# First block of a two-block transformer kernel: the first projections read tokens to which the adaptation shift is not yet added, weight units come in another order, and projections and adaptation parts are placed between the attention heads

## The reference, cut to what matters

```
c_act = silu(c)
ada = c_act @ w_ada + b_ada                    # six parts of 1024
shift_a, scale_a, gate_a, shift_m, scale_m, gate_m = split(ada, 6)
h = rmsnorm(x, g_mix) * (1 + scale_a) + shift_a
gq, gk, gv, gr, gg, mq, mk, mv = split(h @ w_in, ...)   # 256 256 512 512 16 512 512 512
log_a = log_sigmoid(gg @ w_gla_gate + b_gla_gate) / 16
o_gla = rmsnorm(gated_linear_attention(gq, gk, gv, log_a)) * silu(gr)   # 4 heads
o_moba = causal_attention(mq, mk, mv, rel_bias)          # 8 heads of 64
x = x + gate_a * (concat(o_gla, o_moba) @ w_out)
h = rmsnorm(x, g_mlp) * (1 + scale_m) + shift_m
x = x + gate_m * (square(relu(h @ w_ff1)) @ w_ff2)
```

## Time and profile before

| | |
|---|---|
| median of three runs | 1892.06 us |
| the profiled execution | 1894.33 us, its span 1892.2 us |
| PE busy | 1411.1 us (75%) |
| DVE, ACT, POOL busy | 273.4, 237.9, 37.0 us |
| bytes moved | 649.02 MB, mean 343 GB/s |
| first product of `gg` | 41.40 us |
| first scores of the head loop | 145.40 us |
| first product of the output projection | 199.46 us |
| first product of the feed-forward part | 237.60 us |
| last expert | up to the end of the span |

### The profile page before, as it was taken

The page is one execution under the profiler, slowest core; times in us unless marked ns, Lnnn a source line. Parts: engine busy times, 40 slices in busy tenths (PEclk is TensorE's granted clock), DMA queues, the critical chain, the costliest instruction groups (busy, mean ns, idle before and its releaser), DMA issues.

```text
span 1892.2 us, 23896 instructions
## 1 busy us (share of the span) xinstructions
PE 1411.1 (75%) x10492; PEld 824.8 (44%) x10492; DVE 273.4 (14%) x539; ACT 237.9 (13%) x529; POOL 37.0 (2%) x63
## 2 busy tenths in 40 slices
PE   5997899999999776756666676586667658466665
PEld 2674688888857332322323233242232323223222
DVE  1115200003971210010100001000010000101001
ACT  2223122102122310100001000000100001000010
POOL 0000000000110000000000000000000000000000
PEclk8998899999999688677767767767776776776777
DMA  9358233244242899999999999999999999999998
GB/s 350 150 194 343 107 156 155 112 178 155 90 182 93 336 410 427 440 427 437 431 426 438 431 430 435 428 432 436 430 430 434 431 429 439 427 432 435 423 437 344
DMA packets 47207, 649.02 MB, mean 343 GB/s; under 512 B 3816, under 2 KB 6320, under 8 KB 30016
## 3 DMA queue, kind: packets, MB, share of 16 engines
q1 hardware_dynamic: 44112, 643.90, 80.6%
q10 hardware_dynamic: 2848, 3.55, 0.5%
q0 software_dynamic: 208, 1.00, 0.1%
HBM read 647.38 MB, written 1.06 MB: 343 GB/s over the span
## 4 chain that ended last, share of the span: by engine, by line
DMA 49%; PE 20%; DVE 1%; issue 0%; ACT 0%; POOL 0%; SPq 0%; DVEq 0%; PEldq 0%; ACTq 0%; POOLq 0%
DMA ring<-in_w 49%; PE ps L1131 20%; DVE xT L1123 0%; DVE small L1029 0%; DVE arena L1079 0%; DVE arena L1081 0%; DVE arena L1025 0%; ACT L678 0%; ACT L666 0%; POOL arena L446 0%; SPq L359 0%; DVE arena L1098 0%; ACT arena L666 0%; PE ps L1630 0%; ACT arena L719 0%
## 5 line engine op out<-in xcount | busy, mean ns | idle before, releaser
L1131 PE MATMUL ps<-ring,table 128*32 128x352 f32 x4032 | 475.6, 627 | 244.6 <-DMA ring<-in_w 244.4
L1131 PEld LDWEIGHTS ps<-ring,table 128*32 128x32 f32 x4032 | 142.8, 139 | 464.7 <-DMA ring<-in_w 240.2
L1131 PE MATMUL ps<-ring,arena 128*32 128x256 f32 (+1 forms) x2818 | 197.5, 438 | 151.6 <-DMA ring<-in_w 144.0
L1131 PEld LDWEIGHTS ps<-ring,arena 128*32 128x32 f32 (+1 forms) x2818 | 102.9, 125 | 247.5 <-issue 143.1
L1131 PE MATMUL ps<-hT,ring 128*128 128x256 f32 (+1 forms) x912 | 200.4, 382 | 6.8 <-ACT hT L600 3.5
L1131 PEld LDWEIGHTS ps<-hT,ring 128*128 128x128 f32 (+1 forms) x912 | 171.5, 189 | 35.8 <-issue 9.3
L1131 PE MATMUL ps<-arena,ring 128*128 128x256 f32 x768 | 173.0, 387 | 4.4 <-POOL arena L446 2.4
L1131 PEld LDWEIGHTS ps<-arena,ring 128*128 128x128 f32 x768 | 148.4, 194 | 27.8 <-issue 4.2
L1131 PEld LDWEIGHTS ps<-arena,hT 128*128 128x128 f32 x512 | 101.4, 282 | 103.9 <-issue 103.9
L1131 PE MATMUL ps<-arena 32*128 32x256 f32 (+10 forms) x532 | 97.7, 382 | 27.7 <-DVE xT L1123 12.2
L1131 PE MATMUL ps<-arena,hT 128*128 (+1 forms) x512 | 115.6, 366 | 1.8 <-DVEq L1107 1.8
(11 more groups left out here) (213 smaller groups left out, 514.3 us busy)
## 6 DMA issues: line engine op xcount, KB each, us to landing
ring<-in_w SPq DMA_DIRECT2D x76, 5632.0 KB, 32.2
ring<-in_w SPq DMA_DIRECT2D x19, 2816.0 KB, 29.0
ring<-in_w SPq DMA_DIRECT2D x35, 1408.0 KB, 32.7
ring<-in_w_ff SPq DMA_DIRECT2D x8, 4096.0 KB, 13.1
ring<-in_w_ada SPq DMA_DIRECT2D x6, 4096.0 KB, 14.0
ring<-in_w_in SPq DMA_DIRECT2D x4, 4096.0 KB, 17.8
ring<-in_w_out SPq DMA_DIRECT2D x2, 4096.0 KB, 13.9
ring<-in_w_in SPq DMA_DIRECT2D x3, 2048.0 KB, 10.6
```

The source lines that it names most:

```text
L1131: return pe.matmul(o, w, x, start=first, stop=last)
```

## The change

The position of units and of labels (the list `FREED` gives the order in which PE frees the units):

```diff
-UNITS = (["ada0", "ada1", "win_a", "win_b", "win_c", "win_d", "ada2", "ada3", "ada4", "ada5", "wout"]
+UNITS = (["ada1", "win_a", "ada0", "win_v", "ada2", "win_c", "ada3", "win_r", "ada4", "wout", "ada5"]
+FREED = ["ada1", "ada0", "win_a", "win_v", "ada2", "win_c", "win_r", "ada3", "ada4"] + UNITS[9:]
+FILLER = {0: "gr1", 1: "gr2", 2: "gr3", 3: "ada3", 4: "at3", 5: "ada4", 6: "at4"}
-    order = ["rel", "n_in", "ada0", "at0", "ada1", "at1", "gg", "gq0", "gq1", "gk0", "gk1", "z"]
-    order += [f"wf{i}" for i in range(4)] + ["gv0", "gv1"] + [f"gr{i}" for i in range(4)]
-    order += [f"mq{i}" for i in range(4)] + [f"mk{i}" for i in range(4)]
-    order += ["klT", "att0", "att1", "kv0", "kv1", "mv0", "mv1", "o0", "o1", "gs0", "gs1"]
+    order = ["n_in", "ada1", "at1", "gg", "gq0", "gq1", "rel", "ada0", "gk0", "at0", "gk1", "bias", "gv0", "bt", "gv1", "z"]
+    held = {label: set(order[order.index(label) + 1:order.index("bt") + 1]) for label in ("gg", "gq0", "gq1", "gk0", "gk1")}
+    held["gv0"] = {"bt"}
+    order += [f"wf{i}" for i in range(4)] + ["mv0", "mv1", "ada2", "mq0", "at2"]
+    order += [f"mq{i}" for i in range(1, 4)] + [f"mk{i}" for i in range(4)]
+    order += ["klT", "att0", "att1", "kv0", "kv1", "gr0", "o0", "o1", "gs0", "gs1"]
```

SP no longer waits for the small inputs; the values' columns come in two pieces; small inputs have semaphores of their own, and x is waited for only before its squares:

```diff
-            sp.wait_ge(s["small_in"], 16 * 8)
...
-                    sp.wait_ge(s["unit_used"], i - 2)
+                    sp.wait_ge(s["unit_used"], FREED.index(UNITS[i - 3]) + 1)
...
+                if name == "win_v":
+                    sp.dma_start(unit[:, :, n:], rows(T["w_in"], 2576, 512)).then_inc(s["mv_in"], 16)
```

ACT adds the shift to `hT` only after `gk1`, adds a computed bias when it empties the first five banks, and reads `relR` back after them; `gr` is emptied later, inside the head loop:

```diff
-            act.dma_start(rel_dram, rtb).then_inc(s["rel_dram_in"], 16)
-            act.wait_ge(s["rel_dram_in"], 16)
-            act.dma_start(relR, bass.AP(rel_dram.tensor, 0, [[1, P], [384, MH], [1, S]])).then_inc(s["relW_in"], 16)
+            act.dma_start(rel_dram, rtb).then_inc(s["relW_in"], 16)
+            act.wait_ge(s["relW_in"], 16)
+
+            act.wait_ge(s["shift_set"], 1)
+            wait_filled(act, "gk1")
             for c in range(C):
-                act.wait_ge(s["t0_set"], c + 1)
                 A(hT[:, c, :], hT[:, c, :], ACT.Identity, bias=ada[:, c:c + 1]).then_inc(s["hT_set"], 1)
...
+            act.wait_ge(s["gbias_set"], 1)
+            take("gg", ggT, bk("gg")[0:RANK, 0:S], s["ggT_set"], 1, ACT.Identity, bias=gbias[0:RANK, 4:5])
+            for k, label in enumerate(("gq0", "gq1", "gk0", "gk1")):
+                take(label, (gq, gk)[k // 2][:, k % 2 * S:(k % 2 + 1) * S], bk(label)[:, 0:S], s["gqk_set"], k + 1,
+                     ACT.Identity, bias=gbias[:, k:k + 1])
+            act.dma_start(relR, bass.AP(rel_dram.tensor, 0, [[1, P], [384, MH], [1, S]])).then_inc(s["relW_in"], 16)
+            take("gv0", gv[:, 0, :], bk("gv0"), s["gv_set"], 1)
```

PE:

```diff
-            proj("gg", wg, 0, hT, s["hT_set"], n=RANK)
+            proj("gg", wg, 0, hT, s["t0_set"], n=RANK)
             proj("gq0", w, 0, hT)
             proj("gq1", w, P, hT)
+            pe.wait_ge(s["rest_in"], 16 * 4)
+            inc_filled(mm(bk("rel")[0:MH, 0:384], relst, onehot, True, True), "rel")
+            ada_part(0)
             proj("gk0", w, 2 * P, hT)
-            proj("gk1", w, 3 * P, hT, last=True)
+            ada_turn(0)
+            proj("gk1", w, 3 * P, hT)
+            pe.wait_ge(s["shift_set"], 1)
+            wait_emptied(pe, "bias")
+            for c in range(C):
+                mm(bk("bias")[0:32, P:P + RANK], ada[:, c:c + 1].broadcast_to([P, 32]), wg[:, c, :], c == 0, c == C - 1)
+            for c in range(C):
+                for j in range(4):
+                    ins = mm(bk("bias")[32 * j:32 * j + 32, 0:P], ada[:, c:c + 1].broadcast_to([P, 32]),
+                             w[:, c, j * P:(j + 1) * P], c == 0, c == C - 1)
+            finish("bias", ins)
+            wait_unit(pe, "win_v")
+            w = unit_ap("win_v", C, 1024)
+            proj_rows("gv0", w, 0, hT, 0, wait=s["hT_set"])
...
+            pe.transpose(bk("bt")[:, 0:P], rowb[:, 0:P], ident[:, :])
+            inc_filled(pe.transpose(bk("bt")[0:RANK, P:P + 32], rowb[0:32, P:P + RANK], ident[0:32, 0:32]), "bt")
+            proj_rows("gv1", w, 0, hT, 1)
             pe.wait_ge(s["ggT_set"], 1)
...
-            pe.wait_ge(s["relW_in"], 16)
+            pe.wait_ge(s["relW_in"], 32)
             for i in range(4):
                 wait_emptied(pe, f"wf{i}")
...
+            pe.wait_ge(s["mv_in"], 16)
             for st in range(ST):
+                proj_rows(f"mv{st}", w, 512, hT, st, last=(st == 1))
+            ada_part(2)
```

DVE: the order is `ada_rows(1)`, `ada_cols(1)`, the eight chunks of `hT`, then part 0, then two copies each for `bias` and `bt`; the relative table is multiplied by 8 when `wf` is copied. In the head loop scale, add and maximum become one operation:

```diff
-                    V.scalar_tensor_tensor(scb[:, b, 0:P], bk(f"sc{i}")[:, 0:P], HD ** -0.5, relW[:, i, P:2 * P],
-                                           ALU.mult, ALU.add)
...
-                    V.reduce_max(mx[:, 0:1], scb[:, b, 0:P], AX.X)
-                    link(V.reduce_max(mx[:, 1:2], scb[:, b, P:P + S], AX.X))
+                    for st, a, n in ((0, 0, P), (1, P, S)):
+                        ins = V.tensor_tensor_reduce(scb[:, b, a:a + n], bk(f"sc{i}")[:, a:a + n],
+                                                     relW[:, i, P - a:P - a + n], HD ** -0.5, NEG, ALU.add, ALU.max,
+                                                     mx[:, st:st + 1])
```

More of the change, by code:

```diff
@@ L76, in bank_plan @@
             order.append(f"pv{i // 2 - 1}")
-    order += ["n_mlp"] + [f"y{m}" for m in range(C)] + [f"f{m}" for m in range(FF // P)]
-    held = {"n_mlp": {f"y{m}" for m in range(C)}}
+    order += ["n_mlp"] + [f"y{m}" for m in range(C)] + ["ada5", "f0", "f1", "at5"]
+    order += [f"f{m}" for m in range(2, FF // P)]
+    held["n_mlp"] = {f"y{m}" for m in range(C)} | {"ada5"}
     order += [f"g{m}" for m in range(C)] + ["qk0", "n_fin", "qk1"]
@@ L194, in build @@
         h1 = ar(0, 8192, m=FF // P)
-        relst = arena[0:BUCKETS, 4736:4744]
+        relst = arena[0:BUCKETS, 14336:14344]
+        rowb = ar(14344, P + RANK)
+        gbias = small[:, 80:85]
         relW = ex(0, 2048, h=MH)
@@ L517, in take @@
                 empty(act, label)
[L519 to L523, removed]
+            act.wait_ge(s["gbias_set"], 1)
[5 more added lines that the diff above has]
+            take("gv0", gv[:, 0, :], bk("gv0"), s["gv_set"], 1)
+            take("gv1", gv[:, 1, :], bk("gv1"), s["gv_set"], 2)
             wait_filled(act, "z")
@@ L534, in _ @@
             A(tt, tt, ACT.Ln, bias=1.0).then_inc(s["zl_set"], 1)
[L535 to L541, removed]
-            A(flat(sgr), flat(gr), ACT.Sigmoid).then_inc(s["sgr_set"], 1)
             act.wait_ge(s["b_set"], 3)
@@ L587, in _ @@
                           accum_out=rsum[:, 2 * b + st:2 * b + st + 1]).then_inc(s["exp_set"], 1)
+                if i < 3:
+                    gr_take(i + 1)
+                if i == 5:
+                    A(flat(sgr), flat(gr), ACT.Sigmoid).then_inc(s["sgr_set"], 1)
                 if i >= 1:
@@ L757, in ada_cols @@
                 empty(dve, f"at{k}")
-            for k in range(2):
-                ada_rows(k)
-                ada_cols(k)
+            dve.wait_ge(s["x_in"], 16)
+            ada_rows(1)
+            ada_cols(1)
             g0 = VEC["g_mix"][0]
@@ L768, in _ @@
                     .then_inc(s["t0_set"], 1)
+            ada_rows(0)
+            ada_cols(0)
+            dve.sem_inc(s["shift_set"], 1)
+            wait_filled(dve, "bias")
+            V.tensor_copy(rowb[:, 0:P], bk("bias")[:, 0:P])
+            link(V.tensor_copy(rowb[0:32, P:P + RANK], bk("bias")[0:32, P:P + RANK]))
+            empty(dve, "bias")
+            wait_filled(dve, "bt")
+            V.tensor_copy(gbias[:, 0:4], bk("bt")[:, 0:4 * 32].rearrange("p (j q) -> p j q", j=4)[:, :, 0])
+            link(V.tensor_copy(gbias[0:RANK, 4:5], bk("bt")[0:RANK, P:P + 1]))
+            empty(dve, "bt")
+            dve.sem_inc(s["gbias_set"], 1)
             for i in range(4):
                 wait_filled(dve, f"wf{i}")
-                inc_emptied(V.tensor_copy(flat(relW[:, 2 * i:2 * i + 2, :]), bk(f"wf{i}")), f"wf{i}")
+                inc_emptied(V.tensor_scalar(flat(relW[:, 2 * i:2 * i + 2, :]), bk(f"wf{i}"), HD ** 0.5, None, ALU.mult),
+                            f"wf{i}")
             dve.wait_ge(s["zl_set"], 1)
@@ L1153, in _, with ada_part @@
             norm_sum("n_in", sq0, s["sq0_set"])
-            def ada_part(k):
-                wait_unit(pe, f"ada{k}")
-                wait_emptied(pe, f"ada{k}")
+            def ada_part(k, c0=0, c1=C):
+                if c0 == 0:
+                    wait_unit(pe, f"ada{k}")
+                    wait_emptied(pe, f"ada{k}")
                 w = unit_ap(f"ada{k}", C, D)
-                for c in range(C):
+                for c in range(c0, c1):
                     for j in range(4):
@@ L1189, in finish @@
                 bank_done(label)
-            for k in range(2):
-                ada_part(k)
-                ada_turn(k)
+            ada_part(1)
+            pe.wait_ge(s["ident_in"], 16)
+            ada_turn(1)
```

(21 more changed lines are left out.)

110 lines of the change are left out of this document (62 added, 48 removed).

## The result

The changed kernel took 1895.44 us (median of 18 runs), the kernel before beside it 1892.13 us (18 runs). The ratio is 1.0019 with a 95% interval of [1.0011, 1.0026], so by the ratio it is slower by about 3.6 us, where the prediction had it faster by 5.3 us. The profiled execution of the changed kernel has a span of 1895.1 us, 2.9 us more than that of before.

A forecast was written before the change was run, and what follows sets the result against it. PE's products, then waits for experts' matrices, were taken to bound the kernel, so PE's gain counts in full. To the heads -4.5, heads -2.2, output projection +1.4 sum to -5.3 us: 1886.8 us, range 1877.5 to 1892.5.

The forecast's parts named there:

- What bounds the kernel: Whole kernel: PE's products, then waits for experts' matrices; a microsecond PE gains in block one counts in full at the end.
- The first unit and the start: Start: first unit lands at 16.8 us, and the first projection starts at 24.4 instead of 41.40, 17.0 us earlier.
- The new wait: Before wf: read back of the relative table issued at 61.3 us lands at 76.3, so PE stands 7.1 us.
- the rival in which the table lands in time: Before wf: table lands before PE asks, so wait and clock phase fall away; 1877.7 us, chance 0.12.
- Clock: Behind the stand for the table: granted clock at 0.50 for the first work, 2.0 us lost.
- To the heads: From wf at 76.3 us to the first scores, at 140.9 instead of 145.40: -4.5 us.
- The heads: Head loop: steps 0 to 2 shorten, 3 and 5 take 7.4 us each, 4 and 6 about 5.8; -2.2 us.
- The serial rival: Heads: gr copies on ACT stretch steps 1 and 2 to 10.2 us each; +4.5, 1896.6 us, chance 0.08.
- The thinner gains: Heads don't shorten (+2.2) and the cold phase costs 2.8 (+0.8): -2.3, 1889.8 us, chance 0.20.
- Output projection: Up to the feed-forward part: half of part 5 delays the norm by 1.0, its turn adds 0.4; +1.4 us.
- the chances: Own forecast 0.60 with a spread of 3 us, a quarter above -3.8; faster 0.65, same 0.30, slower 0.05.

The follow-up runs named there:

- e1_parts_even: Changed kernel with PE's adaptation parts 3 and 4 in head-loop steps 4 and 6, their turns in 5 and 7; 1884.86 us, ratio 0.9968.
- e7_all: Changed kernel with the edits of e2_long_pieces_moved, e3_table_early, e5_gv1_bank and e8_part5_behind together; 1871.77 us, ratio 0.9896 to the kernel before.
- e3_table_early: Changed kernel with ACT's read back of the relative table issued right after its write has landed; 1885.66 us, ratio 0.9969.
- e5_gv1_bank: Changed kernel with gv1 given the bank of bias instead of that of gk1; 1893.16 us, ratio 1.0010.
- e2_long_pieces_moved: Changed kernel with DVE's reciprocals in steps 2 and 3, its finish in step 5, ACT's sigmoid in step 3; 1883.31 us, ratio 0.9961.
- e4_before_pieces_odd: Kernel before with DVE's reciprocals in steps 3 and 5 and its finish in step 7, beside PE's turns; 1902.70 us, ratio 1.0060.
- e8_part5_behind: Changed kernel with all of adaptation part 5 behind the last two sums of squares; 1894.60 us, ratio 1.0014.
- e9_split_max: Changed kernel with DVE's joined scale-and-maximum in the head loop taken apart again; 1899.03 us, ratio 1.0040.

## Why the prediction was wrong

*What bounds the kernel* held. The shift of the feed-forward part came out at the end nearly in full: +2.3 us and +2.9 in the span for the change, -8.3 and -8.1 for e1_parts_even, -23.8 and -21.5 for e7_all.

*The first unit and the start* held. The unit was there at 17.57 us (16.8 forecast). Its products ran at the full clock (3.66 us, not 5.5), the sums of squares having ended 1.85 us before; I had priced a longer idle time. That this is why the clock stayed up was not tried. The first projection came at 23.66 (24.4). The bias took 2.44 us (2.5).

*The new wait* held in mechanism and size. The read back was issued at 61.38 (61.3), shared packets one to one, and `wf` started at 77.38 (76.3). e3_table_early shows what it cost, about 9 us (0.9969 against 1.0019), and the rival in which the table lands in time is out.

*Clock* was right behind the table, 2.2 us lost (2.0). I had not seen that the stand for `gv1`'s bank, which I had priced at 2.7 us (3.37), has a clock phase of its own: `gv1` took 8.76 us instead of 6.9. But e5_gv1_bank shows that this, too, lay behind the table. To the heads: -3.0 us instead of -4.5; of the difference 1.1 is the later start of `wf` and 0.3 a slower `wf` (5.7 us up to the next row, not 5.4).

*The heads* is the step that failed, and it decides the sign: -2.2 us forecast, +4.2 measured. I wrote that steps 3 and 5 take 7.4 us each and steps 4 and 6 about 5.8. They took 7.3 and 11.6, and 7.5 and 7.1. Steps 0 to 2 came as forecast: the second `pT` stands 14.6 us behind the loop's start, and I had 15.0. Two things were wrong in the failed steps. First, my two figures add up to 13.2 us, which is what a step with a part and a step with a turn took together before (8.3 and 5.0). But the 8.3 us step that I read (165.23 to 173.51) held both the part on PE and the reciprocal on DVE, so the reciprocal was covered there. Put beside a turn it is not covered: a turn's step at the full clock took 3.7 us (161.50 to 165.23 in the timeline of before), and with the 3.35 of the reciprocal or the 3.1 of the finish that makes 7.1 and 6.8, where I had 5.8. Measured were 7.5 and 7.1, 3.0 us more than forecast in the two steps. e1_parts_even and e2_long_pieces_moved bring them together again and gain about 10 and 11 us (from the ratios 0.9968 and 0.9961 against 1.0019); e4_before_pieces_odd parts them in the kernel before and loses 11. Second, I gave a clock price to the stand for the table and none in the heads, where I did not see that PE would stand for 4.9 us. Step 5 alone took 4.2 us more than forecast; of that, part 4 took 2.5 (6.13 instead of 3.66) and the products before it 1.4 (3.12 instead of 1.71). No run separates the clock's share from that of the stand; it is read from these rows.

*The serial rival* ended near the measured time (1896.6 us), but its mechanism did not occur: steps 1 and 2, where `gr` stands, were not longer than forecast. *The thinner gains* put the blame on the heads too, with +2.2 less gain where 6.4 were missing.

*Output projection*: +1.4 forecast up to the feed-forward part with its turn, +1.1 and 0.4 measured. The closeness is in part luck: from the first two sums of squares on it takes 1.9 us more than before (26.8 instead of 24.9), where I had 1.0 for the norm, and the first 48 instructions took 0.9 less (12.54 instead of 13.40). In the chances, the share of my forecast above -3.8 us is nearer to a third than to a quarter: -3.8 is half a spread of 3 us above -5.3.

## What to carry to other kernels

When filler work is moved between the steps of a loop written out by hand, list for each step what is long on every engine: here a step of 8.3 us that hid 3.35 us on another engine, beside one of 5.0, became two steps of over 7 when one of the two was moved. In all traces taken here, each stand of PE of over 4 us in the heads cost twice, itself and the low clock of the work behind it, so the filler belongs where the other engine is longest. And a transfer with a late consumer keeps its early issue even if another edit makes its old place look arbitrary; of two waits in a row the later one has to go first: without the wait for `gv1`'s bank alone nothing was gained that the trace shows, and once the table came in time the same edit gave 5.0 us.

## What the runs showed of the hardware that I had not expected

The price of a wait in clock is not a plain function of its length. In the changed kernel the stands of 3.4 to 6.2 us were each followed by slower work. But the wait of 3.50 us before the feed-forward part in the kernel before was not: 113 instructions took 24.63 us, 0.218 each, and the granted clock was 1.00 from the first of them. In e4_before_pieces_odd the same code behind the same wait started at 0.50:

```profile
242.69 17.50 PE L1131 MATMUL ps<-hT,ring 128*128 128x256 f32 x68 [3.51 <-ACT hT L600]
```

That is 0.257 us for each. Shorter waits gave both results too. In the kernel before, a part behind a wait of 1.90 us took 4.70 us. Waits of up to 2.5 us left both parts at 3.66 us in e1_parts_even, but in e2_long_pieces_moved part 4 took 5.22 us, though no wait in the steps before it was over 2.1 us. How much is lost also differs from one execution to the next for the same instructions: part 4 behind the stand of 4.91 us took 6.13 us in the changed kernel, 6.24 in e5_gv1_bank, 5.31 in e3_table_early and 4.75 in e8_part5_behind, where the code around it is the same. The first three projections took 12.3 to 12.4 us in three executions (the changed kernel, e1_parts_even, e9_split_max) and 10.72 in the other five. Single traces of this kernel can therefore differ by 2 to 3 us in one stage without any edit; the verdicts above rest on the medians, and what is read from the traces on distances of 4 us and more, or on waits.
